# Expert weights exchanged in halves of 1 MB instead of slots of 2 MB

## The reference

```
for grp in range(N_GROUPS):
    wgt = comb * (g_sel == grp)[:, None]
    hg = einsum('nd,edf->enf', hf, w_exp_gate[grp])
    hu = einsum('nd,edf->enf', hf, w_exp_up[grp])
    hid = silu(hg) * hu * wgt.T[:, :, None]
    out = out + einsum('enf,efd->nd', hid, w_exp_down[grp])
```

## Time and profile before

| | |
|---|---|
| median of 3 runs | 1875.35 us |
| profiled execution | 1873.54 us |
| its span | 1871.8 us |
| around the span | 1.7 us |
| PE busy in the span | 1751.0 us (94%) |
| DVE, ACT, POOL busy | 665.4, 470.1, 211.8 us |
| DMA, mean over the span | 336 GB/s |
| first multiplication of an expert step | 914.2 us |
| end of the last one | 1846.2 us |

### The profile page before, as it was taken

One profiled execution on the slowest core, in us unless ns is written; L12 is line 12 of the kernel. 1 busy time (PEld: TensorE's weight loads), 2 busy tenths in 40 slices (PEclk: granted clock), 3 DMA queues, 4 the chain that ended last, 5 costly groups with the idle time before them and its releaser, 6 DMA issues.

```text
span 1871.8 us, 32911 instructions
## 1 busy us (share of the span) xinstructions
PE 1751.0 (94%) x14031; PEld 1106.9 (59%) x14031; DVE 665.4 (36%) x1444; ACT 470.1 (25%) x778; POOL 211.8 (11%) x295
## 2 busy tenths in 40 slices
PE   5689999999989999899899999999999999999997
PEld 2268779988856666799644444445444454444544
DVE  1145554464673544643322222222221222222224
ACT  3044333344531211344411111111111111111114
POOL 1000000011028880343000000000000000000000
PEclk9889999999999999899999999999999999999998
DMA  9989885585388779341799999999999999999993
GB/s 365 419 285 336 295 326 144 188 263 158 131 313 332 302 307 376 100 162 46 320 420 430 428 429 427 430 427 430 427 430 427 430 427 430 427 430 427 430 427 155
DMA packets 124944, 629.64 MB, mean 336 GB/s; under 512 B 10469, under 2 KB 78493, under 8 KB 83360
## 3 DMA queue, kind: packets, MB, share of 16 engines
q1 hardware_dynamic: 118974, 608.45, 80.9%
q0 software_dynamic: 5120, 17.44, 2.7%
q10 hardware_dynamic: 754, 2.33, 0.3%
HBM read 618.65 MB, written 9.56 MB: 336 GB/s over the span
## 4 chain that ended last, share of the span: by engine, by line
PE 42%; DMA 13%; DVE 1%; issue 1%; SPq 0%; ACT 0%; POOL 0%; DVEq 0%; POOLq 0%; ACTq 0%
PE pb L2681 24%; DMA ring<-in_w_exp_gate 13%; PE pb L2655 4%; PE pb L2661 2%; PE pb L2689 2%; PE pb L2032 2%; PE pb L2033 2%; PE pb L2034 1%; PE pb L2662 1%; PE pb L2570 0%; DVE xt L1830 0%; SPq L502 0%; PE pb L2731 0%; PE pb L2577 0%; PE pb L2728 0%
## 5 line engine op out<-in xcount | busy, mean ns | idle before, releaser
L2681 PE MATMUL pb<-ring,pj 128*64 128x512 f32 x2048 | 460.0, 602 | 23.9 <-DMA ring<-in_w_exp_gate 23.0
L2681 PEld LDWEIGHTS pb<-ring,pj 128*64 128x64 f32 x2048 | 149.2, 138 | 298.8 <-issue 294.7
L2032 PE MATMUL pb<-ht_parts,ring_parts 128*128 128x264 f32 x1056 | 309.5, 293 | 7.3 <-DVE ring_parts L1304 6.2
L2033 PE MATMUL pb<-ring_parts 128*128 128x264 f32 x1056 | 302.1, 286 | 0.0
L2034 PE MATMUL pb<-ring_parts 128*128 128x264 f32 x1056 | 301.8, 286 | 0.0
L2689 PE MATMUL pb<-ring,pj 128*64 128x512 f32 x1024 | 223.3, 594 | 0.0
L2032 PEld LDWEIGHTS pb<-ht_parts,ring_parts 128*128 128x128 f32 x1056 | 202.0, 191 | 24.3 <-issue 16.0
L2033 PEld LDWEIGHTS pb<-ring_parts 128*128 128x128 f32 x1056 | 202.0, 191 | 0.0
L2034 PEld LDWEIGHTS pb<-ring_parts 128*128 128x128 f32 x1056 | 200.9, 190 | 0.0
L1304 DVE TENSOR_TENSOR ring_parts<-ring,ring_parts 128x2048 fp32r<-128x2048 f32 x50 | 114.6, 2292 | 173.9 <-ACT ring_parts L789 173.8
L2689 PEld LDWEIGHTS pb<-ring,pj 128*64 128x64 f32 x1024 | 72.2, 137 | 138.9 <-issue 136.9
(11 more groups left out here) (474 smaller groups left out, 1959.2 us busy)
## 6 DMA issues: line engine op xcount, KB each, us to landing
ring<-in_w_exp_gate SPq DMA_DIRECT2D x64, 2048.0 KB, 15.2
ring<-in_w_exp_up SPq DMA_DIRECT2D x64, 2048.0 KB, 17.2
ring<-in_w_exp_down SPq DMA_DIRECT2D x64, 2048.0 KB, 15.7
ring<-in_w_ada SPq DMA_DIRECT2D x32, 2048.0 KB, 14.8
ring<-in_w_in SPq DMA_DIRECT2D x24, 2048.0 KB, 9.4
pj<-in_w_ada SPq DMA_DIRECT2D x32, 1024.0 KB, 7.8
ring<-in_w_ada_final SPq DMA_DIRECT2D x16, 2048.0 KB, 13.0
ring<-in_w_out SPq DMA_DIRECT2D x8, 2048.0 KB, 8.6
```

The costliest lines, as they stand in the source:

```text
L2032: pe.matmul(out, hi[:, k, :], ht_lo[:, k, :], start=(k == 0), stop=False)
L2033: pe.matmul(out, lo[:, k, :], ht_hi[:, k, :], start=False, stop=False)
L2681: last = pe.matmul(pb[step // 2][SLOT * q:SLOT * q + SLOT, :], xg[:, k, SLOT * q:SLOT * q + SLOT], w[q][:, j, :], start=(k == 0), stop=(k ...
```

## The change

Each slot is now loaded and used in two halves of 1 MB. `half_slot(s, part)` is the first or second 2048 floats of a slot. `expert_load` issues four DMAs of 1 MB for a step instead of two of 2 MB, in the order: first half for expert 0, first half for expert 1, second half for expert 0, second half for expert 1. A half of gate or up is 4 of the 8 rows of a partition, a run of 8 KB. A half of down is columns 0 to 1023 or 1024 to 2047 of both rows of a partition, two runs of 4 KB.

```
+                for part in range(2):
+                    for q in range(2):
+                        s = moe_slot(step, q)
+                        if freed is not None:
+                            sp.wait_ge(S(("m_half", "m_step")[part]), freed)
+                        elif s < MIX_SLOTS:
+                            sp.wait_ge(S("out_ps"), 8 + 2 * OUT_SLOTS.index(s) + 2)
+                        else:
+                            sp.wait_ge(S("out_ps"), KD)
...
+                        if step < 4:
+                            at = (step % 2 * 2 + part) * 4
+                            src = src[:, at:at + 4, :]
+                        else:
+                            at = step % 2 * 2
+                            src = src[:, at:at + 2, part * (D // 2):(part + 1) * (D // 2)]
+                        sp.dma_start(half_slot(s, part).rearrange("p (k f) -> p k f", f=src.shape[2]), src)\
+                            .then_inc(half_full(s, part)[0], 16)
```

`moe_step` waits for the two first halves, does the 8 multiplications that use them (4 blocks of rows for gate and up; output banks 0 and 1 for down), raises the new semaphore `m_half`, waits for the two second halves, does the other 8 and raises `m_step`:

```
+                for part in range(2):
+                    for q in range(2):
+                        full, before = half_full(moe_slot(step, q), part)
+                        pe.wait_ge(full, (t * 2 + step // 3 + 1) * 16 + before)
+                    w = [half_slot(moe_slot(step, q), part) for q in range(2)]
+                    if step < 4:
+                        for j in range(4):
+                            k = step % 2 * 8 + part * 4 + j
...
+                    else:
+                        for n in range(2 * part, 2 * part + 2):
...
+                            if step == 5 and n % 2 == 0:
+                                last.then_inc(S("m_yb"), 1)
+                    last.then_inc(S(("m_half", "m_step")[part]), 1)
```

More of the change, by code:

```diff
@@ L277, in slot, with half_slot, half_full @@
             return ring[:, s * RING:(s + 1) * RING]
+        def half_slot(s, part):
+            return ring[:, s * RING + part * (RING // 2):s * RING + (part + 1) * (RING // 2)]
+        def half_full(s, part):
+            if part == 0 and s < MIX_SLOTS:
+                return S(f"ring_full{s}"), out_loads(4 + OUT_SLOTS.index(s))
+            return S(f"m_full{s}{'ab'[part]}"), 0
         def weight_tile(mem, s, m):
@@ L486, in expert_load @@
             def expert_load(pair, step, freed=None):
[L488 to L503, removed]
+                for part in range(2):
[7 more added lines that the diff above has]
+                            sp.wait_ge(S("out_ps"), KD)
+                        w = (w_exp_gate, w_exp_up, w_exp_down)[step // 2]
+                        src = w[0].rearrange("g e a b -> (g e) a b")[bass.ds(pair * 2 + q, 1)]
+                        src = src.rearrange("o (p k) f -> p (o k) f", p=P)
+                        if step < 4:
[6 more added lines that the diff above has]
+                            .then_inc(half_full(s, part)[0], 16)
             for step in range(3):
@@ L618, in _ @@
             pool.wait_ge(*once("sv_evac"))
-            pool.dma_start(scratch, sv_row).then_inc(S("sv_store"), 16)
-            pool.wait_ge(S("sv_store"), 16)
+            pool.dma_start(scratch, sv_row).then_inc(S("sv_moved"), 16)
+            pool.wait_ge(S("sv_moved"), 16)
             for v in range(6):
                 pool.dma_start(svt[:, v, :], scratch[v * NS:(v + 1) * NS, :].rearrange("b (h d) -> (b h) d", d=RD))\
-                    .then_inc(S("sv_in"), 16)
-            pool.wait_ge(S("sv_in"), 96)
+                    .then_inc(S("sv_moved"), 16)
+            pool.wait_ge(S("sv_moved"), 112)
             vr, vw, vk, vv, vkk, vb = (svt[:, i, :] for i in range(6))
@@ L1024, in gn_sqrt @@
                 act.activation(rb[:, :, g], rb[:, :, g], ACT.Sqrt).then_inc(S("gn_act"), 1)
-            act.wait_ge(S("sv_store"), 16)
+            act.wait_ge(S("sv_moved"), 16)
             def eight(bank):
@@ L1181, in moe_act @@
                     act.wait_ge(S("m_step"), t * STEPS + 2)
-                    act.activation(sg, pb[0][:], ACT.Silu).then_inc(S("m_sg"), 1)
-                    act.wait_ge(S("m_wt"), t + 1)
-                    act.copy(pwt[:, 0:NP_], pb[7][:, 0:NP_]).then_inc(S("m_wte"), 1)
+                    act.activation(sg, pb[0][:], ACT.Silu).then_inc(S("m_act"), 1)
+                    act.wait_ge(S("m_turn"), t * 2 + 1)
+                    act.copy(pwt[:, 0:NP_], pb[7][:, 0:NP_]).then_inc(S("m_act"), 1)
                     moe_gather_out(ps * GA + i * 4 + 4, 0)
-                    act.wait_ge(S("m_hp"), t + 1)
-                    act.copy(hid_t, pb[6][:].rearrange("p (c s) -> p c s", s=P)).then_inc(S("m_ht"), 1)
+                    act.wait_ge(S("m_turn"), t * 2 + 2)
+                    act.copy(hid_t, pb[6][:].rearrange("p (c s) -> p c s", s=P)).then_inc(S("m_act"), 1)
                     for n in range(4):
-                        if n < 3:
-                            act.wait_ge(S("m_yb"), t * 3 + n + 1)
+                        if n % 2 == 0:
+                            act.wait_ge(S("m_yb"), t * 2 + n // 2 + 1)
+                        elif n == 1:
+                            act.wait_ge(S("m_half"), t * STEPS + 6)
                         else:
@@ L1852, in moe_dve @@
                     moe_add(t)
-                    dve.wait_ge(S("m_wt"), t + 1)
+                    dve.wait_ge(S("m_turn"), t * 2 + 1)
                     for q in range(2):
@@ L1856, in moe_dve @@
                         last = dve.tensor_copy(w_slot[r, :], pb[6][r, q:q + 1])
-                    last.then_inc(S("m_ws"), 1)
+                    last.then_inc(S("m_dve"), 1)
                     moe_dispatch(ps * 17 + i + 1, i + 1)
-                    dve.wait_ge(S("m_ws"), t + 1)
-                    dve.wait_ge(S("m_sg"), t + 1)
+                    dve.wait_ge(S("m_dve"), t * 2 + 1)
+                    dve.wait_ge(S("m_act"), t * 3 + 1)
                     dve.wait_ge(S("m_step"), t * STEPS + 4)
                     dve.scalar_tensor_tensor(out=sg, in0=sg, scalar=w_slot, in1=pb[1][:], op0=ALU.mult, op1=ALU.mult)\
-                        .then_inc(S("m_hid"), 1)
+                        .then_inc(S("m_dve"), 1)
                     moe_gather_out(ps * GA + i * 4 + 4, 1)
@@ L2671, in moe_step @@
             def moe_step(t, step):
[L2673 to L2687, removed]
-                            for q in range(2):
[L2689 to L2692, removed]
@@ L2693, in moe_step @@
-                last.then_inc(S("m_step"), 1)
+                for part in range(2):
[6 more added lines that the diff above has]
+                            k = step % 2 * 8 + part * 4 + j
+                            for q in range(2):
+                                last = pe.matmul(pb[step // 2][SLOT * q:SLOT * q + SLOT, :], xg[:, k, SLOT * q:SLOT * q + SLOT],
+                                                 w[q][:, j * FF:(j + 1) * FF], start=(k == 0), stop=(k == KD - 1))
+                    else:
+                        for n in range(2 * part, 2 * part + 2):
+                            for j in range(2):
+                                c, at = (step - 4) * 2 + j, j * (D // 2) + n % 2 * BANK
+                                for q in range(2):
+                                    last = pe.matmul(pb[2 + n][SLOT * q:SLOT * q + SLOT, :], hid_t[:, c, SLOT * q:SLOT * q + SLOT],
+                                                     w[q][:, at:at + BANK], start=(c == 0), stop=(c == 3))
+                            if step == 5 and n % 2 == 0:
+                                last.then_inc(S("m_yb"), 1)
+                    last.then_inc(S(("m_half", "m_step")[part]), 1)
@@ L2697, in moe_pe @@
                 if not isinstance(ps, int):
-                    pe.wait_ge(S("m_hid"), ps * NPAIRS)
+                    pe.wait_ge(S("m_dve"), ps * (2 * NPAIRS))
                     pe.wait_ge(S("m_xga"), ps * XG)
@@ L2731, in moe_pe @@
                         last = pe.transpose(pb[7][:, c * P:(c + 1) * P], disp[:, c, :], ident[:])
-                    last.then_inc(S("m_wt"), 1)
+                    last.then_inc(S("m_turn"), 1)
                     moe_step(t, 3)
-                    pe.wait_ge(S("m_wte"), t + 1)
+                    pe.wait_ge(S("m_act"), t * 3 + 2)
                     pe.wait_ge(S("m_dp"), n + 2)
                     moe_gather(0)
-                    pe.wait_ge(S("m_hid"), t + 1)
+                    pe.wait_ge(S("m_dve"), t * 2 + 2)
                     for c in range(4):
                         last = pe.transpose(pb[6][:, c * P:(c + 1) * P], sg_in_rows[:, c, :], ident[:])
-                    last.then_inc(S("m_hp"), 1)
+                    last.then_inc(S("m_turn"), 1)
                     moe_gather(1)
-                    pe.wait_ge(S("m_ht"), t + 1)
+                    pe.wait_ge(S("m_act"), t * 3 + 3)
                     pe.wait_ge(S("m_add"), t * KD + KD)
```

## The result

The changed kernel takes 1890.24 us (median of 4 runs, 1887.71 to 1892.44) against 1875.32 us for the kernel before beside it (1875.16 to 1878.07): the ratio is 1.0074, 95% interval 1.0056 to 1.0093. It is 14.9 us slower. The execution that was profiled was the slowest of the four, 1892.44 us with a span of 1890.7, 18.9 us over the profiled one of before.

The account below looks back on a forecast made before the run. The prediction took DMA throughput as the bound, PE 4% behind. Stream plus 20.0 us, start 3.0 won, transfers ending 16.9 later, PE 12.3 later; 1873.54 + 12.3 = 1885.8, median 1887.6, rounded to 1887; range 1873 to 1903 us.

Parts of the forecast that it names:

- Part 1, smaller packets: Expert weight stream: shorter runs make smaller packets, 184 loads take 922.0 us instead of 902.0, 20.0 more; pair 60.1 us.
- Part 2, the start: Start of the expert stage: earlier orders remove the pauses between 919 and 935 us, 3.0 us won, nothing later.
- Part 3, the end: Last pair: PE ends 4.5 us after the last transfer instead of 9.1, at 1858.5 against 1846.2, plus 12.3 us.
- The sum: Whole kernel: 1873.54 + 12.3 = 1885.8 us for the profiled execution; median 1.81 above, 1887.6, rounded to 1887.
- Part 4: SP and PE: 12 more DMA issues and 12 more waits a pair, and merged semaphores, cost nothing.
- Packets at no cost: Rival on the weight stream: packets of 8 and 4 KB flow like 16 KB, 8.1 us won, 1867 us; chance 0.19.
- The case with only 8 KB free: Rival's variant: 8 KB packets free, 4 KB at half an 8 KB packet, 4.1 us won, 1871 us.
- A fixed time for each DMA: Rival on the saturated stream: 0.1 us for each of 184 more DMAs adds 18 us, 1906 us; chance 0.09.
- The clock: Rival on PE: more idle time drops the granted clock; four drops a pair cost 44 us, 1931 us; chance 0.09.

Follow-up runs that it names:

- e1: Kernel before, whole 2 MB loads, but gate and up in runs of 8 KB and down in runs of 4 KB: 1900.35 us, ratio 1.0127.
- e12: Kernel before, each 2 MB load given as two 1 MB DMAs over even and odd partitions, runs of 16 KB: 1873.72 us, ratio 0.9992.
- e3: Kernel before, whole 2 MB loads, but all expert weights in runs of 4 KB: 1913.30 us, ratio 1.0196.
- e6: Changed kernel, but SP orders both halves of a slot only when the whole step before is done: 1892.85 us, ratio 1.0094 to the kernel before.
- e8: Kernel before, halved only in steps 3 and 4 of the first pair and 0, 3, 5 of the last: 1874.83 us, ratio 0.9997.
- e9: Kernel before, halved only in first pair's steps 3 to 5, second's 0 and 1, last's all but 4: 1870.11 us, ratio 0.9975.
- e4: Kernel before, whole 2 MB loads, but all expert weights in runs of 2 KB: 1975.82 us, ratio 1.0529.
- e7: Changed kernel, but PE waits for both halves of both slots before a step's first multiplication: 1895.46 us, ratio 1.0101 to the kernel before.
- e10: Changed kernel with down loaded whole in 16 KB runs, gate and up still in halves: 1882.92 us, ratio 1.0038 to the kernel before.
- e2: Kernel before, each 2 MB load given as two 1 MB DMAs over partitions 0 to 63 and 64 to 127: 2779.77 us, ratio 1.4833.
- e5: Changed kernel run again as it is: 1889.78 us against 1874.07 for the kernel before, ratio 1.0085.
- e11: Changed kernel with gate and up loaded whole in 16 KB runs, down still in halves: 1888.20 us, ratio 1.0060 to the kernel before.

## Why the prediction was right

The forecast was 1887 us, 12.3 us slower; measured were 14.9 in the medians. The stage grew by 16.2 us.

**Part 1, smaller packets.** Right in mechanism and nearly in size. e1 (runs without halves) and e12 (more loads without short runs) separate the two, and only the runs cost. The pair was put at 60.13 us (922.0 us for 184 loads) and is 60.25: 1.8 us over 15.3 pairs. 8 KB was priced at 0.3106 us and is 0.3103; 4 KB at 0.159 and is 0.1598, which over 2048 packets an engine (128 halves of 16) is 1.6 of those 1.8. By e3's 410 GB/s the Trainium skill's figure for 4 KiB rows ("DMA: Bandwidth & Descriptors", the section on the iDMA fabric), 408.7, was a little nearer than my 412.

**Part 2, the start.** Right that the pauses go and that nothing else comes of early orders: e6 puts it at 3.1 us against 3.0. What the prediction didn't say, and e8 beside e9 showed, is that this gain lasts only with halves in the steps that follow, until the queue has its lead; the change has them.

**Part 3, the end.** PE ends 1863.4 - 1857.9 = 5.5 us behind the transfers, not 4.5, because the last half was used 1.8 us after the last byte, 1 us having been allowed. It is a gain of 3.6 us against before instead of 4.6. The last transfer itself ended at 1857.9, not near 1854.

**The sum.** PE's last step ended at 1863.4 and was put at 1858.5. Of these 4.9 us 1.0 lies ahead of the stage, 1.8 are the packets, 1.0 the landing; 1.1, between the start of the stream and its end, I can't assign. Behind the stage come 1.7 us more, 1.2 of them with the lower clock, of which the prediction had nothing. So the profiled execution, 1892.44 us, is 6.6 us over the 1885.8 that the sum gives for it. The median lies only 2.6 us over the 1887.6; that it is so near is in part luck, as the profiled execution was the slowest of its four, 2.2 us over their median, where the one of before lay 1.8 under its own.

**Part 4** held: PE's step in two parts costs nothing in the chain (7.04 us for the 32 records of a step that doesn't wait), and in the middle PE waits for weights alone, but for ten waits of 0.2 us for DVE that the kernel before has too.

**The rivals.** Packets at no cost: out, by e1, e3 and e4; the 430 GB/s of 2 us in the earlier trace rows was too short a window to go by. (The case with only 8 KB free should have read 3.8 us won, 8.1 less the 4.3 of its sum.) A fixed time for each DMA: out, by e12. The Trainium skill's 341 GB/s for 1 MB ("DMA: Bandwidth & Descriptors", "Measured" under "Bandwidth") did not hold for a queue like this one, where loads of 1 MB ran at 429; no run here has such a load by itself. The clock: it went the other way. In the changed kernel's middle it is 1.00, and no step takes 8.7 us, while the kernel before had four in its chain and e7 eight. All of them follow a wait of more than 2 us for gate weights, though not every such wait brings one (4 of 8 before, 8 of 13 in e7), and e10's five follow waits of 2.7 us for down weights; the halves' waits of up to 1.4 us brought none. In the middle that is worth nothing, as the stream is the bound. Whether the lower clock behind the stage (27.3 to 27.5 us for that part in this kernel, e2, e4, e5 and e8 to e11, 24.7 to 25.6 in the others) comes from the change is open: e2 and e4, which have no halves, show it, and e6 and e7, which have them, don't.

## What to carry to other kernels

Where the DMA engines are full, count packets before anything else: here each cost some 9 ns of its engine, so a split that shortens the contiguous runs lengthens the whole stream, and a split that keeps them is free, if it doesn't go by lower and upper partitions (e2). Earlier orders and finer waits can only win where the stream pauses or ends; look for these places in windows of the DMA share, and halve there alone, with all the steps up to where the queue has its lead.

## What was not expected of the hardware

Two loads of 64 neighbouring partitions each ran at 218 GB/s with all engines shown busy, the same two by even and odd partitions at 429. The Trainium skill ("DMA: Bandwidth & Descriptors", "Rules for kernel authors") says of transfers to disjoint halves of the partitions that they serialize and bring nothing. These runs agree that they bring nothing, and show that for the lower and upper half the price is half the bandwidth.
